# Attention's buffer dissolved into idle places, one tick later, and a ninth slot for experts' rows

## The reference, cut to what matters

```python
for l in range(DEPTH):
    h = rmsnorm(x, norm_mix_g[l]); proj = h @ w_in[l]
    ...                                   # conv, attention, ssm, group norms
    x = x + y @ w_out[l]
    x = x + memory_cross_attention(rmsnorm(x, ...), rmsnorm(mem, ...), w_mq[l], w_mkv[l], w_mo[l])
    x = x + peer_ffn(rmsnorm(x, norm_ffn_g[l]), peer_wq[l], peer_sub_keys[l], peer_u[l], peer_v[l])
return rmsnorm(x, final_norm_g)

# peer_ffn, for each token and each of 8 heads
q = xc @ w_q;  sc = q against 2 x 128 sub keys;  top 16 of each;  best 16 of the 256 sums -> 16 experts
act = gelu(u_e . xc)                      # u_e: row of peer_u, 1024 wide
out = sum(gate * act * v_e)               # v_e: row of peer_v, 1024 wide
```

## Time and profile before

| | |
|---|---|
| median of 3 runs | 1749.54 us |
| the profiled execution | 1749.91 us, span 1748.1 us |
| granted clock, mean | 0.985 |
| PE busy | 1593.1 us (91%) |
| DVE busy | 1206.1 us (69%) |
| ACT, POOL busy | 597.1 us, 588.3 us (34% each) |
| DMA | 680.39 MB, mean 389 GB/s |
| gathers of experts' rows | 536.90 MB, 512 instructions |

### The profile page before, as it was taken

One profiled execution on the slowest core, in us unless ns is written; L12 is line 12 of the kernel. 1 busy time (PEld: TensorE's weight loads), 2 busy tenths in 40 slices (PEclk: granted clock), 3 DMA queues, 4 the chain that ended last, 5 costly groups with the idle time before them and its releaser, 6 DMA issues.

```text
span 1748.1 us, 19658 instructions
## 1 busy us (share of the span) xinstructions
PE 1593.1 (91%) x6652; PEld 970.2 (55%) x6652; DVE 1206.1 (69%) x3337; ACT 597.1 (34%) x1445; POOL 588.3 (34%) x527
## 2 busy tenths in 40 slices
PE   7999989999899999998989989999999997777777
PEld 7878866545547777643645647644655643223232
DVE  6721389986886667997646567998556577667665
ACT  3132232463334232155323233155333223222222
POOL 0000143344333332343334333344343344433432
PEclk9999999999999999999999999999999999999999
DMA  9546599999999999999999999999999999999996
GB/s 378 195 145 247 225 378 421 418 383 421 421 406 403 421 421 421 421 420 414 421 421 420 419 422 417 419 367 397 421 422 420 421 422 421 422 421 421 421 422 274
DMA packets 94580, 680.39 MB, mean 389 GB/s; under 512 B 10488, under 2 KB 10768, under 8 KB 12304
## 3 DMA queue, kind: packets, MB, share of 16 engines
q0 software_dynamic: 73728, 536.90, 74.7%
q1 hardware_dynamic: 20752, 142.23, 20.1%
HBM read 678.05 MB, written 1.05 MB: 388 GB/s over the span
## 4 chain that ended last, share of the span: by engine, by line
PE 37%; DMA 29%; DVE 13%; ACT 4%; issue 2%; POOL 0%; DVEq 0%; ACTq 0%
DMA slots<-expert_rows,expert 29%; PE bank L777 22%; PE bank L394 8%; DVE slots L1608 5%; PE bank L562 2%; PE bank L765 2%; PE bank L762 2%; ACT diag L1194 1%; DVE sg L1231 1%; DVE att L1485 1%; DMA ring<-w_blocks 1%; DVE coef L1231 1%; DVE x L1231 0%; DVE cands L1589 0%; PE bank L705 0%
## 5 line engine op out<-in xcount | busy, mean ns | idle before, releaser
L777 PE MATMUL bank<-slots,diag 128*128 128x512 f32 x1916 | 910.2, 611 | 130.5 <-ACT diag L1194 125.9
L886 POOL DMA_INDIRECT slots<-expert_rows,expert x512 | 586.4, 1145 | 1136.7 <-PE bank L777 882.7
L1608 DVE CUSTOM_DVE_ANT_0 slots<-slots,htok 128x1024 f32<-128x1024 f32 x512 | 626.3, 1223 | 359.8 <-DMA slots<-expert_rows,expert 356.1
L777 PEld LDWEIGHTS bank<-slots,diag 128*128 128x128 f32 x1916 | 348.8, 193 | 546.3 <-issue 324.0
L1207 ACT ACTIVATE gel<-dot 128x2 f32<-128x2 f32 (+1 forms) x258 | 52.5, 204 | 698.5 <-DVE dot L1608 693.6
L394 PEld LDWEIGHTS bank<-hT,ring 128*128 128x128 f32 x1696 | 207.0, 194 | 47.3 <-issue 47.0
L1194 ACT ACTIVATE diag<-ident,coef 128x128 f32<-128x128 f32 x479 | 168.2, 394 | 189.0 <-DVE coef L1231 183.1
L394 PE MATMUL bank<-hT,ring 128*128 128x128 f32 x1696 | 207.9, 277 | 2.8 <-DMA ring<-w_blocks 2.8
L1231 DVE SCALAR_TENSOR_TENSOR coef<-gel,ginv,gexp 128x2 f32<-128x2 f32 (+1 forms) x258 | 54.3, 211 | 48.4 <-ACT gel L1207 45.5
L1207 ACT ACT_TABLE_LOAD x66 | 84.7, 1283 | 1.2
L1231 DVE SCALAR_TENSOR_TENSOR sg<-pad,prm,sg 128x128 f32<-128x128 f32 x240 | 71.3, 341 | 0.0
(11 more groups left out here) (274 smaller groups left out, 1513.6 us busy)
## 6 DMA issues: line engine op xcount, KB each, us to landing
ring<-w_blocks SPq DMA_DIRECT2D x99, 1024.0 KB
slots<-w_blocks SPq DMA_DIRECT2D x23, 1024.0 KB, 7.0
slots<-expert_rows,expert POOLq DMA_INDIRECT x512
kept<-w_blocks SPq DMA_DIRECT2D x4, 1024.0 KB, 13.3
keys<-w_blocks SPq DMA_DIRECT2D x2, 1024.0 KB, 10.8
prm<-small SPq DMA_DIRECT2D x2, 768.0 KB
x<-x_rows SPq DMA_DIRECT2D x2, 512.0 KB, 11.6
slots<-mem_rows SPq DMA_DIRECT2D x1, 1024.0 KB, 8.0
```

Of the source, the lines that this page charges most:

```text
L777: last = mm(bank[h][:, :], diag[:, i % DIAGS, :], slots[:, n % SLOTS, D + h * 512:D + (h + 1) * 512], start=m == 0, stop=n == end)
L886: nc.gpsimd.indirect_dma_start(slots[:, n % SLOTS, :], None, experts_d, bass.IndirectOffsetOnAxis(ap=idx[q % 2][:, k:k + 1], axis=0),).the ...
L1608: v.tensor_tensor_reduce(out=slots[:, s, 0:D], in0=slots[:, s, 0:D], in1=htok[:, ph % 2, :], scale=1.0, scalar=0.0, op0=ALU.mult, op1=ALU.add,
```

## The change

`att_` is gone. Its tensors lie in places that hold nothing at that time, other ones for chunk 0 (`homes`' first entry) than for later chunks. The 8.2 KB a partition make room for a ninth slot, which is also a tenth place for the weights of chunk 0. Because `sn`, `sp`, `stay` and `aT` now lie in `pr_` for chunks 1 to 3, where the state-space model's products were, attention begins one tick later there, with two new waits, and what comes behind it is one tick later too (`LATER`, group sums, mixing, `WQ_AT`, the set-up of layer 1). SP loads chunk 1's block u into `W_` only after the memory attention of chunk 0, since `mE` now lies there. `TAKER` keeps its pattern of 8.

```diff
-WIDE = 9
+WIDE = 10
-SLOTS = 8
+SLOTS = 9
-LATER = [0] + [5] * (NST - 1)
+LATER = [0] + [6] * (NST - 1)
 def att_tick(ci, g, step):
-    return BEGIN[ci] + 31 + 4 * g + step if ci else ...
+    return BEGIN[ci] + 32 + 4 * g + step if ci else ...
-WQ_AT = [[89 + 2 * h ...], [94 + h * 5 // 2 ...], [94 + 4 * h ...], [94 + 4 * h ...]]
+WQ_AT = [[89 + 2 * h ...], [95 + h * 5 // 2 ...], [95 + 4 * h ...], [95 + 4 * h ...]]
-        pr_ = sb("products", [P, 2048])
+        pr_ = sb("products", [P, 2 * S + 2 * S + 2 * (S + 1) + 512])
-        att_ = sb("att", [P, 2 * S + 2 * S + 2 * (S + 1) + 512])
+        sns, sps, aTs = ([home[:, i:i + 512].rearrange("p (h n) -> p h n", h=2) for home, i in homes]
+                         for homes in ([(flat, 0)] + [(pr_, 0)] * (NST - 1), [(flat, 512)] + [(pr_, 512)] * (NST - 1),
+                                       [(flat, 1024)] + [(pr_, 1538)] * (NST - 1)))
+        left = [... for home, i in [(htok[:, 0, :], 0)] + [(pr_, 1024)] * (NST - 1)]
+        mE = W_[:, 0:1024].rearrange("p (h m) -> p h m", h=MH)
+        rowT = hT[:, :, :].rearrange("p t s -> p (t s)")
+        mPT = rowT.rearrange("p (h m s) -> p h m s", h=MH, m=2)
+        pqT = qT[:, :, :].rearrange("p (b t) s -> p b t s", b=2)
+        squares, squares1, squaresM = rowT, htok[:, 1, :], W_[:, ST * TP:ST * TP + D]
 # group_sums 51 -> 52, groups 52 -> 53, mixed (53, 55, 57) -> (54, 56, 58) for ci > 0
 # SP, ahead of chunk 1's block u
-                    full(("conv sum", 0))
+                    full(("mem t", 1, 0))
 # ScalarE, attention
+                        if g == 0 and ci:
+                            eng.wait_ge(y_used, 3 * (ci + 1))
 # VectorE, attention, g == 0
+                        if ci:
+                            full(("ssm y", ci))
 # VectorE, set-up of layer 1, ahead of `near`
+                if l:
+                    full(("mem t", 1, 1))
-SETUP_TICK = [..., lambda n: 71 + n // 4 if n < 75 else 92 + (n - 75) // 4]
+SETUP_TICK = [..., lambda n: 72 + n // 4 if n < 75 else 92 + (n - 75) // 4]
```

More of the change, by code:

```diff
@@ L74 @@
 NEVER = 10 ** 9
-LATER = [0] + [5] * (NST - 1)
+LATER = [0] + [6] * (NST - 1)
 def att_tick(ci, g, step):
-    return BEGIN[ci] + 31 + 4 * g + step if ci else (30, 31, 32, 32, 33, 34, 35, 36)[step] + 3 * g
+    return BEGIN[ci] + 32 + 4 * g + step if ci else (30, 31, 32, 32, 33, 34, 35, 36)[step] + 3 * g
 KEYS_AT = [[13 + i * 27 // 18 for i in range(18)] + [40 + i for i in range(8)] + [53 + i for i in range(6)],
@@ L95 @@
 SSM_LATER = [6, 0, 0, 0]
-WQ_AT = [[89 + 2 * h for h in range(PH)], [94 + h * 5 // 2 for h in range(PH)],
-         [94 + 4 * h for h in range(PH)], [94 + 4 * h for h in range(PH)]]
-TAKER = ["vector" if (n < 16 or 104 <= n < 144) and n % SLOTS in (2, 4, 7)
+WQ_AT = [[89 + 2 * h for h in range(PH)], [95 + h * 5 // 2 for h in range(PH)],
+         [95 + 4 * h for h in range(PH)], [95 + 4 * h for h in range(PH)]]
+TAKER = ["vector" if (n < 16 or 104 <= n < 144) and n % 8 in (2, 4, 7)
          or n < NG - PER and 44 <= n % PER < 60 and n % 4 == 2 else "tensor" for n in range(NG)]
@@ L226, in build @@
         cfg = [[home[:, i * 512:(i + 1) * 512].rearrange("p (t r n) -> p t r n", t=ST, r=2) for i in range(2)]
-               for home in (att_, W_)]
+               for home in (htok[:, 0, :], W_)]
         sq = W_[:, 0:KT * P].rearrange("p (t s) -> p t s", t=KT)
-        pr = pr_[:, :].rearrange("p (b i t r s) -> p b i t r s", b=2, i=2, t=2, r=2)
+        pr = pr_[:, 0:2048].rearrange("p (b i t r s) -> p b i t r s", b=2, i=2, t=2, r=2)
         moT = pr_[:, 0:1024].rearrange("p (t s) -> p t s", t=KT)
@@ L232, in build @@
         ys, cacc, sgl, lnt = va, sg, uT, qT[:, 0:CT, :]
[L233 to L240, removed]
         flat = slots[:, :, :].rearrange("p s n -> p (s n)")
         memX = [flat[:, 0:2048].rearrange("p (m d) -> p m d", m=2),
-                pr_[:, :].rearrange("p (m d) -> p m d", m=2)]
+                pr_[:, 0:2048].rearrange("p (m d) -> p m d", m=2)]
         memH = [flat[:, 2048:4096].rearrange("p (t s) -> p t s", t=KT),
@@ L246, in build @@
         outs = [W_[:, 0:1024], pr_[:, 0:1024]]
+        sns, sps, aTs = ([home[:, i:i + 512].rearrange("p (h n) -> p h n", h=2) for home, i in homes]
+                         for homes in ([(flat, 0)] + [(pr_, 0)] * (NST - 1), [(flat, 512)] + [(pr_, 512)] * (NST - 1),
+                                       [(flat, 1024)] + [(pr_, 1538)] * (NST - 1)))
+        aTs = [t.rearrange("p h (k s) -> p h k s", k=2) for t in aTs]
+        left = [home[:, i:i + 2 * (S + 1)].rearrange("p (h n) -> p h n", h=2)
+                  for home, i in [(htok[:, 0, :], 0)] + [(pr_, 1024)] * (NST - 1)]
+        mE = W_[:, 0:1024].rearrange("p (h m) -> p h m", h=MH)
[3 more added lines that the diff above has]
+        squares, squares1, squaresM = rowT, htok[:, 1, :], W_[:, ST * TP:ST * TP + D]
         bank = [ctx.enter_context(nc.psum_tensor(f"bank{i}", [P, 512], F32)) for i in range(8)]
@@ L518, in attention @@
                                 last = nc.tensor.transpose(bank[6][:, (2 * h + k) * P:(2 * h + k + 1) * P],
-                                                           sp[:, h, lo + k * P:lo + (k + 1) * P], ident[:, :])
+                                                           sps[ci][:, h, lo + k * P:lo + (k + 1) * P], ident[:, :])
                         last.then_inc(filled[6], 1)
@@ L534, in attention @@
                                 last = mm(bank[7][rr:rr + AD, h * P:(h + 1) * P], vt[:, k, hh * AD:(hh + 1) * AD],
-                                          aT[:, h, k, :], start=k == 0, stop=k == c, skip_group_check=True)
+                                          aTs[ci][:, h, k, :], start=k == 0, stop=k == c, skip_group_check=True)
                         last.then_inc(filled[7] if g % 2 else aT_used, 1)
@@ L539, in group_sums @@
                 at = BEGIN[ci]
-                yield at + (51 if ci else 47)
+                yield at + (52 if ci else 47)
                 fill(4, ("sums", ci))
@@ L911, in root_ahead, with root_of_x @@
                 act(ahead[:, :], epsb[:, :], ACT.Sqrt)
-            def root_of_x(ci):
+            def root_of_x(ci, first=False):
                 c = ci % NC
-                step(act(squares, x[:, c, :], ACT.Square, accum_out=ss[:, :]))
+                step(act(squares1 if first and ci == 1 else squares, x[:, c, :], ACT.Square, accum_out=ss[:, :]))
                 act(root[:, :], ss[:, :], ACT.Sqrt, scale=1.0 / D, bias=epsb[:, :]).then_inc(norm_root, 1)
@@ L937, in mix @@
                     eng.wait_ge(x_added, 2 * (ci - 1))
-                root_of_x(ci)
+                root_of_x(ci, True)
                 yield at + 2
@@ L997, in attention @@
                             full(("att o", g // 2 - 1, ci))
-                        done(act(aT[:, :, 0:1 + c, :], src[:, :, 0:1 + c, :], ACT.Copy), name)
+                        done(act(aTs[ci][:, :, 0:1 + c, :], src[:, :, 0:1 + c, :], ACT.Copy), name)
                     g = step_
@@ L1003, in attention @@
                         src = full(name)[:, :].rearrange("p (h n) -> p h n", h=2)[:, :, lo:S]
-                        act(sn[:, :, lo:S], src, ACT.Sigmoid, scale=-AD ** -0.5)
-                        done(act(sp[:, :, lo:S], src, ACT.Sigmoid, scale=AD ** -0.5), name)
+                        if g == 0 and ci:
+                            eng.wait_ge(y_used, 3 * (ci + 1))
+                        act(sns[ci][:, :, lo:S], src, ACT.Sigmoid, scale=-AD ** -0.5)
+                        done(act(sps[ci][:, :, lo:S], src, ACT.Sigmoid, scale=AD ** -0.5), name)
                     g = step_ - 1
@@ L1037, in groups @@
                 at = BEGIN[ci]
-                yield at + (52 if ci else 48)
+                yield at + (53 if ci else 48)
                 name = ("sums", ci)
                 done(act(groot[:, 0:2], full(name)[:, 0:2], ACT.Sqrt, bias=epsb[:, :]), name)
-                yield at + (52 if ci else 48)
+                yield at + (53 if ci else 48)
                 name = ("conv sum", ci)
@@ L1127, in mem_keys @@
                     for m in range(2):
-                        step(act(squares, memX[l][:, m, :], ACT.Square, accum_out=mss[:, m:m + 1]))
+                        step(act(squaresM, memX[l][:, m, :], ACT.Square, accum_out=mss[:, m:m + 1]))
                 act(mroot[:, :], mss[:, :], ACT.Sqrt, scale=1.0 / D, bias=epsb[:, :]).then_inc(mem_root, 1)
@@ L1480, in attention @@
                     yield att_tick(ci, g, 2)
+                    sn, sp, stay = sns[ci], sps[ci], left[ci]
                     if g == 0:
+                        if ci:
+                            full(("ssm y", ci))
                         step(v.memset(stay[:, :, S:S + 1], 1.0))
@@ L1493, in mixed @@
                 at = BEGIN[ci]
-                for i, (first, tick) in enumerate(((2, 53), (6, 55), (0, 57)) if ci else ((2, 49), (6, 50), (0, 52))):
```

(3 more changed lines are left out.)

## The result

The changed kernel takes 1758.43 us (median of 5 runs, 1755.43 to 1759.95), the kernel before 1748.38 us beside it: ratio 1.0051, interval 1.004 to 1.0062. By the medians that is 10 us slower, by the ratio 8.9 us (0.0051 of some 1750); the ratio isn't the quotient of these two medians. All later runs are compared by their ratios to the kernel before, run beside each of them; each ratio is uncertain by about 0.0012, so a difference between two of them by some 3 us. Forecast was 1747.2 us, 1742.5 to 1755.0, with 0.37 for faster and 0.22 for slower: the measured time lies above the range, and on the other side. The profiled execution took 1759.95 us, its span is 1758.2 us, 10.1 us over that of before.

The account below looks back on a forecast made before the run. From the gathers on, DMA bytes were taken to set the end, so only DMA idle time counts. Start +8.0, ninth slot -10.3, tick 0 and longer weight queue 0 gave -2.3 us: 1747.2 us, range 1742.5 to 1755.0.

Parts of the forecast that it names:

- start: Weights before the first expert: changed places of the last blocks delay the first gathers; +8.0 us, bounds +6 and +10.5.
- tick: Attention and what follows it moved one tick later against experts that stay; cost 0, bounds -2 and +3 us.
- ninth slot: DMA gets one gather further ahead in each compute-bound stretch; -10.3 us in sum, bounds 0 and -13.0.
- The three gathers: Start: only gathers 0 to 2 issued until 226.7, before 0 to 5; three later, 3 x 2.49 = 7.5 us.
- gate's block: Start: chunk 1's block gate, issued beside gathers 0 and 1, may delay wq7 by up to 2.49 us; 0.5 taken.
- A: Stretch 345 to 400 us, paced by VectorE: 4.2 us of DMA idle, ninth slot to save 2.8.
- B: Stretches 485 to 505 and 540 to 565 us, paced by TensorE: 3.6 us idle, slot to save 2.8.
- C: Stretch 780 to 820 us: 0.9 us of DMA idle, all of it to be saved by the ninth slot.
- D: Stretch 1140 to 1220 us: 8.3 us of DMA idle, ninth slot to save 2.8.
- the tail: Stretch 1705 to 1720 us: 1.0 us of DMA idle, all to be saved by the ninth slot.
- a tick between is 0.8 us of slack: Last phase: VectorE busy 1.7 us a tick against 2.49, used for putting the moved tick's cost at 0.
- The slower one: Rival: ninth slot eaten by the expert pipeline, only C and the tail give something; +6.1 us, 1755.6, chance 0.25.

Follow-up runs that it names:

- the other pair: Changed kernel with chunk 0's weights round nine places (ratio 0.998), against the kernel before with only the moved tick, eight slots (1.0027): 0.0047, 8.2 us between them.
- the run with the blocks held: Changed kernel with chunk 1's blocks gate, q0 and q1 issued only once wq6 has been multiplied: 1755.9 us, ratio 1.0035.

## Why the prediction was wrong

*The accounting held.* From before to after: start +12.4, tick at eight slots +4.7, ninth slot under the tick -7.9 (all three as differences of ratios): +9.2, and 8.9 measured (0.0051). The sum proves less than it seems to: with the slot's 8.2 us from the other pair it closes by itself, since each step then begins at the kernel where the last one ended. What it tests is that the slot is worth the same with the late start (7.9) as without (8.2). The prediction's form, DMA idle added up over places, was right; three of its terms were mis-sized. Against the forecast of -2.3 the start was off by 4.4, the tick by 4.7 and the slot by 2.4 us.

*The start, +8.0 with a bound of +10.5: measured 12.4.* The three gathers and their cause were right, and so was "paid in full". The step that failed here is the one on gate's block: I saw that it would be issued beside gathers 0 and 1, saw that wq7 stands behind experts 0 and 1 on TensorE, and took 0.5 us of a possible 2.5. With q0, which I had left out and which is issued before dot 0 too, it was 4.7. Dot 1 came 3.3 us later, and the engine that then stood still was TensorE, so the clock term that I left out came too: the granted clock of TensorE was 0.77 from 221.6 to 224 and 0.61 from 224 to 227, and wq7's first half took 3.11 us instead of 1.95. The first row below is that half; the second, over a longer stretch, takes in the standstill behind wq7:

```profile
224.00:227.00 3.00, 3.00 (x18) 3.00 (x17) 0.95 (x1) 0.00 (x0) 0.00 (x0) 0.61 0.06 25
222.00:235.00 13.00, 8.95 (x44) 6.63 (x42) 2.03 (x6) 0.36 (x2) 2.86 (x4) 0.80 0.32 110
```

The low end was chosen because TensorE "comes to expert 0 only after wq6". That spare time was about half a microsecond (dot 1 came 3.3 us later and TensorE waited 2.85), and the bound should have been the transfers plus what follows a standstill. The rule that an engine takes turns between its queues (the Trainium skill, "DMA: Bandwidth & Descriptors", "Queues, rings and completion order") pointed to a late gather, and the run with the blocks held shows them to be the cause; whether the turns are taken packet by packet no run here shows.

*The ninth slot, -10.3: measured -7.9 with the tick, -4.9 without.* One gather's time for each stretch was right for A and B under the tick (2.9, 2.8), and C gave it too (2.4, where I had taken 0.9 as all the idle there was). D, where the idle is largest, gave 0.5 instead of 2.8, and the tail at most 0.2 of its 1.0. The rule "one gather further ahead at the end" takes for granted that the lead is cashed, that is, that compute behind the stretch runs faster than the gathers arrive. I didn't show that it does there, and no run tests it. Why D differs from A, whose work is the same, stays open: nine, eight and seven slots give 8.9, 9.4 and 7.8 us there, and the kernels with eight slots alone spread from 7.6 to 10.4.

*The tick, 0 with a bound of +3: measured 4.7 on the kernel before, 0.5 on nine slots.* The step that failed is "a tick between is 0.8 us of slack", taken from the last phase, where no other work runs. It was about VectorE's sum of work, which is unchanged. In the compute-bound stretches there is no such slack: A, B and C idle 5.3 us more with the tick alone. Which work meets which experts was moved, and I didn't ask which. That the new wait for "ssm y" costs nothing was right; the row stands again without a wait:

```profile
346.66 0.60 DVE L1239 SCALAR_TENSOR_TENSOR va<-uT,prm,bank 128x128 f32<-128x128 f32 x2
```

Why the tick behind attention makes the stretches worse, by which meeting of strands, was not settled. The number of activation table loads (ScalarE loading the table of a function) is the same, 149 before, after and with the tick alone, so more of them is not the reason.

*The rest.* TensorE hardly waited for the ring: 2.1 us in two waits, 2.8 before, as forecast. The tail's dip in the rate went, but the last dots gained 0.2 us and not 1.0, and the dip was gone with eight slots and the moved tick as well (421 GB/s from 1716.36 to 1726.36), so it wasn't the slot.

```profile
PE bank L399 <- DMA ring<-w_blocks: 2.1, 2, 1.6
```

*The rivals.* The slower one named the right side but put the loss in the ninth slot, which it left nearly without a gain in A, B and D, and took the start as in the forecast and the tick at nothing; its 1755.6 fell short as well.

## What to carry to other kernels

When buffers are lent to another use, write down the order in which they come back against the order in which the first user asks for them; a pool that is larger by one, filled in a circle, can turn that order over. Here it cost 12 us, more than the ninth buffer gave; turning it the other way gave another 2.5 to 3 us. A transfer that is moved beside the first one on a critical chain can cost more than the delay of the data, since what follows a standstill comes on top (here dot 1 came 3.3 us later and wq7 ended 4.7 us later), so its upper end belongs in the sum unless a row shows that it is covered. And slack that is read in one phase doesn't hold for another: work that is moved by one tick should be priced in the stretches that have none.

## What the hardware did that was not expected

In the changed kernel TensorE waited 2.85 us in front of expert 0, and sixteen 128x128 matmuls behind it took 3.11 us instead of 1.95; after the wait of 8.75 us four 128x512 matmuls took 3.78 us instead of 1.88. From 235 to 240 its granted clock was 0.50, the lower of its two levels (1.2 GHz), after it had all but stood still from 231:

```profile
235.00:240.00 5.00, 0.30 (x1) 0.30 (x2) 2.55 (x8) 0.96 (x3) 4.08 (x4) 0.50 0.99 416
```

So these two standstills of TensorE were paid twice: once as waiting, once as slower matmuls behind them (0.6 and 1.2 us behind the first, 1.9 behind the second).
